# Three stages of split weights at six distances from the turned tokens

## The reference, cut to what matters

```python
for layer in range(DEPTH):
    hn = rmsnorm(h, mix_norm_pre[layer])
    proj = jnp.einsum('bsd,de->bse', hn, w_in[layer])
    ...
    mix = jnp.einsum('bse,ed->bsd', jnp.concatenate([y_pool, y_na], axis=-1), w_out[layer])
    h = h + rmsnorm(mix, mix_norm_post[layer])
    hn = rmsnorm(h, ffn_norm_pre[layer])
    if layer % 2 == 0:
        f = swiglu(hn, dense_w_gate[j], dense_w_up[j], dense_w_down[j])
    else:
        f = moe_swiglu(hn, moe_router[j], moe_w_gate[j], moe_w_up[j], moe_w_down[j])
    h = h + rmsnorm(f, ffn_norm_post[layer])
```

## Time and profile before

| what | us |
|---|---|
| median of three runs (1324.23 to 1327.34) | 1325.38 |
| the profiled execution | 1325.36 |
| its span | 1323.4 |
| PE busy in the span | 1288.7 |
| DVE busy | 416.8 |
| ACT busy | 277.2 |

### The profile page before, as it was taken

The page is one execution under the profiler, slowest core; times in us unless marked ns, Lnnn a source line. Parts: engine busy times, 40 slices in busy tenths (PEclk is TensorE's granted clock), DMA queues, the critical chain, the costliest instruction groups (busy, mean ns, idle before and its releaser), DMA issues.

```text
span 1323.4 us, 31100 instructions
## 1 busy us (share of the span) xinstructions
PE 1288.7 (97%) x14401; PEld 794.7 (60%) x14401; DVE 416.8 (31%) x595; ACT 277.2 (21%) x430; POOL 108.9 (8%) x240
## 2 busy tenths in 40 slices
PE   8989999999999899999999999999999999999996
PEld 7878999999989773354353354345353355336433
DVE  5786555555576861030020040030030031021011
ACT  4556444444463640000000000000000000000101
POOL 4132400000000305500000000000000000000000
PEclk9999999999999999999999999999999999999999
DMA  9536955555544199999999999999999999999994
GB/s 312 206 113 199 285 195 195 196 195 195 191 148 169 57 409 428 426 424 382 427 425 427 425 425 424 426 425 425 425 426 425 427 425 424 425 427 423 425 425 177
DMA packets 66869, 443.50 MB, mean 335 GB/s; under 512 B 4505, under 2 KB 10657, under 8 KB 42161
## 3 DMA queue, kind: packets, MB, share of 16 engines
q1 hardware_dynamic: 64592, 433.58, 80.5%
q0 software_dynamic: 2144, 7.90, 2.1%
HBM read 439.36 MB, written 2.10 MB: 334 GB/s over the span
## 4 chain that ended last, share of the span: by engine, by line
PE 84%; DVE 8%; DMA 3%; ACT 2%; SPq 1%; issue 1%; ACTq 0%; DVEq 0%
PE psum L1052 38%; PE psum L1061 18%; PE psum L710 8%; PE psum L712 8%; PE psum L711 8%; DMA unit<-in_moe_w_down 3%; PE psum L996 2%; DVE w_lo L1393 2%; PE psum L1007 1%; DVE prob L1534 1%; DVE negmax L1525 1%; ACT prob L1261 1%; DVE prob L1522 1%; PE psum L731 1%; SPq L371 1%
## 5 line engine op out<-in xcount | busy, mean ns | idle before, releaser
L1052 PE MATMUL psum<-unit,xT 128*32 128x448 f32 x5376 | 507.0, 539 | 0.1
L1052 PEld LDWEIGHTS psum<-unit,xT 128*32 128x32 f32 x5376 | 174.4, 110 | 327.4 <-issue 325.2
L1061 PE MATMUL psum<-unit,hid 128*32 128x256 f32 x4704 | 259.1, 379 | 3.1 <-DMA unit<-in_moe_w_down 3.1
L1061 PEld LDWEIGHTS psum<-unit,hid 128*32 128x32 f32 x4704 | 151.4, 110 | 108.3 <-issue 5.3
L1710 DVE TENSOR_TENSOR hidp<-hid,psum 128x448 f32<-128x448 f32 x42 | 38.5, 917 | 535.4 <-PE psum L1052 535.4
L1393 DVE TENSOR_TENSOR w_lo<-ring,w_hi 128x2048 fp32r<-128x2048 f32 x72 | 166.1, 2312 | 119.0 <-ACT w_hi L1164 118.7
L710 PE MATMUL psum<-hT_hi,w_hi 128*128 128x256 f32 x656 | 182.4, 278 | 1.6 <-DVE qT L1500 1.6
L711 PE MATMUL psum<-hT_lo,w_hi 128*128 128x256 f32 x656 | 181.3, 276 | 0.0
L712 PE MATMUL psum<-hT_hi,w_lo 128*128 128x256 f32 x656 | 181.3, 276 | 0.0
L1164 ACT ACTIVATE w_hi<-ring 128x2048 fp32r<-128x2048 f32 x72 | 137.4, 1912 | 63.7 <-PE psum L712 52.3
L710 PEld LDWEIGHTS psum<-hT_hi,w_hi 128*128 128x128 f32 x656 | 123.3, 188 | 3.5 <-DVE qT L1500 1.8
(11 more groups left out here) (243 smaller groups left out, 936.0 us busy)
## 6 DMA issues: line engine op xcount, KB each, us to landing
unit<-in_moe_w_gate SPq DMA_DIRECT2D x64, 1792.0 KB, 32.6
unit<-in_moe_w_up SPq DMA_DIRECT2D x64, 1792.0 KB, 27.0
unit<-in_moe_w_down SPq DMA_DIRECT2D x64, 1792.0 KB, 32.1
ring<-in_dense_w_gate SPq DMA_DIRECT2D x8, 2048.0 KB, 9.1
ring<-in_dense_w_up SPq DMA_DIRECT2D x8, 2048.0 KB, 9.1
ring<-in_dense_w_down SPq DMA_DIRECT2D x8, 2048.0 KB, 8.3
ring<-in_w_in SPq DMA_DIRECT2D x6, 2048.0 KB, 8.5
ring<-in_w_out SPq DMA_DIRECT2D x4, 2048.0 KB, 7.9
```

The costliest lines, as they stand in the source:

```text
L1052: ins = mm(bank(half, s)[quad(j)], xT[:, s, dt, :], w[:, at:at + FJ], start=dt == 0, stop=dt == DT - 1)
L1061: ins = mm(down_out[s][quad(j)], e[:, half, s, t, :], w, start=half == t == 0 and s != 2, stop=half == 1 and t == FT - 1, skip_group_check ...
```

## The change

`w_hi` and `w_lo` become lists of three separate tensors. Ahead of each a gap is placed, chosen so that the stage lies a given number of bytes behind the turned tokens, modulo 1,024: 96, 160 and 224 for the stages of `w_hi`, and 320, 448 and 544 for those of `w_lo`. The six gaps are 32, 64, 64, 96, 128 and 96 bytes. The assertion holds the turned tokens at 128 bytes modulo 1,024, where they stood before. `uT`, `pt23`, `h`, `gpost`, `win_b`, `router_sb`, `rows` and `cols` move up by 480 bytes in all, and `spare` takes up the difference, so that `hs` and all behind it stay where they were. No instruction is added, taken away or moved on any engine.

```diff
-        w_hi = sb("w_hi", [P, STAGE, 8 * C2], F32R)
-        w_lo = sb("w_lo", [P, STAGE, 8 * C2], F32R)
+        HT_AT = 128
+
+        def staged(name, apart):
+
+            out_ = []
+            for k, n in enumerate(apart):
+                gap = (HT_AT + n - plan_top[0]) % 1024
+                sb(f"{name}_gap{k}", [P, gap // 4])
+                out_.append(sb(f"{name}{k}", [P, 8 * C2], F32R))
+            return out_
+
+        w_hi = staged("w_hi", (96, 160, 224))
+        w_lo = staged("w_lo", (320, 448, 544))
...
-        assert plan_top[0] <= nc.sbuf_usable_end
+        assert plan_top[0] <= nc.sbuf_usable_end and addr["hT_hi"] % 1024 == addr["hT_lo"] % 1024 == HT_AT
...
-                hi, lo = w_hi[:, n % STAGE, :], w_lo[:, n % STAGE, :]
+                hi, lo = w_hi[n % STAGE][:, :], w_lo[n % STAGE][:, :]
...
-                return w_hi[:, n % STAGE, :], w_lo[:, n % STAGE, :]
+                return w_hi[n % STAGE][:, :], w_lo[n % STAGE][:, :]
```

More of the change, by code:

```diff
@@ L716, in split_half @@
                 pe.wait_ge(split_ready, n + 1)
-                return w_hi[:, n % STAGE, :], w_lo[:, n % STAGE, :]
+                return w_hi[n % STAGE][:, :], w_lo[n % STAGE][:, :]
             def open_half(n, dsts, half):
-                w = [a.rearrange("p (t n) -> p t n", t=DT) for a in (w_hi[:, half % STAGE, :], w_lo[:, half % STAGE, :])]
+                w = [a.rearrange("p (t n) -> p t n", t=DT) for a in (w_hi[half % STAGE][:, :], w_lo[half % STAGE][:, :])]
                 pe.wait_ge(hT_hi_ready, 4 * n + 4)
```

## The result

The changed kernel takes 1336.11 us (median of four runs, 1332.82 to 1336.45), the kernel before 1324.81 us (median of four). The ratio is 1.0067, with a 95% interval of 1.0046 to 1.0088: 0.67% slower, some 9 to 11 us. The median lies 2 us above the predicted range, which ended at 1334 us; the lowest of the four runs, 1332.82 us, lies inside it.

The account below looks back on a forecast made before the run. PE alone bounds the dense part; the end hangs on transfers beginning at 452.33 us. The profiled execution's 1325.36 us plus zero for the change gave a forecast of 1325.5 us, range 1317 to 1334 us.

Parts of the forecast that it names:

- The bound: Dense part, 119 to 381 us: nothing but PE sets its time, busy for 261.90 of 262.00 us.
- The reading of the expert part: From about 500 us: the end hangs on transfers beginning at 452.33 us; changes before that move the end one for one.
- The step that failed: Matmuls ahead of the first unit: the distance between weights and tokens costs zero, since a 512-byte change left 113.3 ns.
- the case of none: Narrow matmuls: distance has no period because it has no effect, against a period of 512 bytes or a part of it.
- the prediction's own sign: Narrow matmuls, by stage: the prediction is wrong if a stage's pace leaves 113 ns by over 2 ns.
- The bound above: Matmuls ahead of the first unit, all slow: 6.9 us for narrow ones plus 1.3 us for wide ones, 8.2 us.
- a fifth of a narrow stage at most: Mixing parts: share of a narrow stage's cost given to their about 430 narrow matmuls and fills, only partly on the chain.
- Rival 1: Dense part: some stages fall to the slow pace; two of three cost 4.6 us, giving 1330 us; chance 0.33.
- Rival 2: PE matmuls: new distances part the two streams and remove excess; a third of 15.9 us, giving 1320 us; chance 0.27.
- Rival 3: PE matmuls: the change does nothing, the excess being fixed or dependent on timing alone; 1325.5 us; chance 0.40.
- The reading for timing: `open_half`, layers 0 and 1: 118.1 and 113.1 ns with one distance, so how the streams fall in time decides.

Follow-up runs that it names:

- experiment 3: Changed kernel with all high-weight stages at 64 bytes and all low-weight stages at 320; 1325.80 us, ratio 1.0005 to the kernel before.
- experiment 6: Changed kernel with high-weight stages at 64, 64, 320 bytes and low ones at 320, 576, 576; 1325.27 us, ratio 1.0007 to the kernel before.
- experiment 2: Changed kernel with high and low weights at one distance per stage, 96, 160 and 224 bytes; 1335.17 us, ratio 1.0063 to the kernel before.
- experiment 1: Changed kernel with all six weight stages back at 64 bytes, the other tensors still moved by 480; 1325.05 us, ratio 0.9987 to the kernel before.
- experiment 8: Changed kernel with turned tokens and all weight stages moved up 32 bytes, keeping 64 bytes between them; 1328.60 us, ratio 1.0024 to the kernel before.
- experiment 5: Changed kernel with high and low weights at one distance per stage, 192, 288 and 320 bytes; 1332.76 us, ratio 1.0053 to the kernel before.
- experiment 9: Changed kernel with high weights back at 64 bytes, low ones still at 320, 448 and 544; 1331.26 us, ratio 1.0042 to the kernel before.

## Why the prediction was wrong

**The bound** was right. The dense part is set by PE's steps alone: the run of matmuls grew by 8.6 us and so did the part. The reading of the expert part was right too: the first unit's issue moved by 9.85 us, the span by 10.6.

**The step that failed** is this one: "I take zero: the one change of distance that the rows do show within a run of matmuls, by 512 bytes, does nothing." A shift of 512 bytes could not tell. Experiments 3 and 6 show that 64, 320 and 576 bytes are as one, so the only comparison that the trace offered was between two places that these runs find equally good. The prediction named this itself ("If there is a period, it is 512 bytes or a part of it, or there is none") and then took the case of none. The measured cost of the term is 4.7 ns for each of 1536 narrow matmuls and 3.6 ns for each of 384 wide ones in the dense part, 8.6 us where I had zero. By the prediction's own sign, a pace that leaves 113 ns by over 2 ns, it was wrong in all three stages.

**The bound above** was too small: 8.2 us, for a measured 9.85 us ahead of the first unit. I had taken the slowest paces seen, 117.8 and some 231.7 ns, as the worst. Stages reach 119.0 ns in the change and 119.9 in experiment 2, and a wide step has 232.5 on the average; my 231.7 was the mean step plus a difference of shown durations, which is no difference of steps. The mixing parts gave 1.3 us (0.41 of it within the scatter; the 0.86 of the second repeats, since from the last dense matmul to the first unit's issue it is 71.1 to 71.2 us in the kernel before and in experiments 1, 3 and 8, and 71.9 to 72.0 in the change and in 2 and 6), for which I had named "a fifth of a narrow stage at most", under 0.5 us. They hold 576 narrow matmuls ahead of the first unit, and not about 430: 288 in each layer, 192 of them in a row. The first 192 of layer 1 alone, worked out from their starts, went from 113.9 to 118.9 ns on the average, which is 1.0 us.

**Rival 1**, some stages falling to the slow pace, is what happened, but in three stages of three, and in stage 0 to a pace beyond it. Its reason, that the kernel already stood in the best pace and another draw was more likely to lose, held: of the eight distances modulo 256 that the runs tried for high and low together, one (64) was found fast. **Rival 2** found no support: 107 ns was never seen. Its premise, that the excess over half the slow clock's step belongs to the distance, isn't shown for the 6 ns that are left at 113.3. **Rival 3**, the forecast, has fallen.

**The reading for timing** was right as far as it went. I had seen `open_half` at 118.1 and 113.1 ns on the same addresses. Experiments 5, 6 and 9 show this same pair of paces inside one kernel. The mistake was to see timing and distance as alternatives. As the runs stand, the distance limits which paces are there, and something that differs between halves and between executions picks one; that it is the timing of the two streams is argued, not shown.

**What the pages say.** The page "SBUF — State Buffer" of the Trainium skill (Who interferes with whom) calls PE's two read ports independent and says that PE never waits on anyone. The last is said of other engines, and no run here tests it. But the prediction drew from the page that the distance costs nothing, and this the runs contradict: the same 1920 matmuls need 262.1 or 270.7 us according to the distance of the two operands, with no other engine's work changed. This measurement decides.

**What stays open.** Why 64 is good and 96 is not; whether 192 for all weights, which was slow at 117.8 ns only next to bad stages, is good by itself (117.8 is the slow pace of the good places, but stage 2 of the change has it too); what picks the pace; and what part of the slower step is of the load and what of the stream. All stages at 192 would settle the second and wasn't tried. No version here beats the kernel before.

## What to carry to other kernels

When matmuls run back to back and each has its own weight load, the places of the still and the moving operand are a parameter of the kernel: here they were worth 4% of each narrow step, and places 256 bytes apart (64, 320 and 576; 192 and 448) did the same. Keep the distance the same in all buffers of a ring and note it in the code, since an unrelated tensor ahead of them can shift it, and a good buffer behind a bad one can be slow too (experiments 5 and 9). A comparison in the trace between places that are a multiple of the likely period apart says nothing on the distance; and before taking an execution's pace for the kernel's, look at how far the executions spread.

## What the runs showed of the hardware

- The narrow step is 113.3 ns at 64 / 64 (113.3 to 114.1 at 64 / 192), modulo 256, or 117.8 ns at 64 / 64, and 116.7 to 119.9 ns at the seven others tried for both weights. The wide step within a half is 228.8 ns at 64 and at 256 bytes, and 232.3 to 234.2 at 96, 128, 160, 192 and 288. It has a second pace as well: 229.8 ns at 64 / 320 in experiments 6 and 9, 228.8 in experiment 3.
- At 64, 320 and 576 bytes the pace is kept over the border between halves, and through a whole dense part (experiment 6), but a single longer step of 0.22 us changed it there; a stretch of wide matmuls changed it once for the better (experiment 8) and in experiment 5 always for the worse. Behind a half with other distances it may be kept or not (experiment 9).
- At the granted clock of 0.50 a wide step was 0.43 us, and 229 ns at 1.00, some 14 ns more than half of it: this excess is seen at the full clock alone.
